# Running the small attention heads of a two-block transformer kernel in pairs on the two halves of the array

## The chip, the cores and the metric

One core of a Trainium2 chip runs the whole program. The metric is device time in microseconds of one execution; the median of three runs of the kernel before is 4096.61 us.

## What is computed

The first block (two mixer layers with attention, gated linear attention and a convolution) stays as it is. The change lies in the second block, in its three kinds of attention heads over 512 positions with heads 64 wide, and in the gates that weigh the three branches afterwards:

```python
def banded_attention(q, k, v, bias_tab, window, sink=None):      # kind B, window 128, with a sink
    s = einsum(q, k) * D ** -0.5 + bias; p = softmax(masked s); return einsum(p, v)

def second_block(...):
    h = rms_norm(x, norm_mix[layer])
    proj = h @ w_in[layer]
    aq, ak, av, bq, bk, bv, cq, ckv, cg, mg = jnp.split(proj, points, axis=-1)
    oa = diff_attention(aq, ak, av, lam, bias_a)      # kind A: 4 heads, p[0] - lam * p[1]
    ob = banded_attention(bq, bk, bv, bias_b, B_WINDOW, sinks[layer])   # kind B: 8 heads, 2 key heads
    oc = nsa_attention(cq, kc, vc, ksel, ckv[:, :, 3], kwin, ckv[:, :, 5], cg, bias_c)
                      # kind C: 8 heads, 2 key heads; g0*o_cmp + g1*o_sel + g2*o_win
    branches = jnp.stack([oa, ob, oc], axis=0)
    y = jnp.einsum('nbsm,nmd->bsnd', branches, w_branch[layer])
    gate = jax.nn.sigmoid(mg.reshape(B, S, N_BRANCH, D_MODEL))
    x = x + jnp.sum(gate * y, axis=2) @ w_out[layer]
```

All is float32. The projections take their operands as two rounded parts each (three products per tile); the scores and the products with the values are plain float32.

## The kernel before

The second block's projections for keys and values come first, then the small compression network, then the stage named "heads", then the branch products (`w_branch_2`), the output projection and the feed-forward part.

**The units of the heads stage.** The stage is a list `heads2` of 160 units, 40 for each of four rounds `i`. A unit is 128 query rows (`qt` 0 to 3) of one head against the keys that these rows may see: 128, 256, 384 or 512 keys for the kinds A (`c0` and `c1`, its two halves), C `sel` and C `win`; 128 or 256 for B; 31 compressed keys for C `cmp`. In a round stand 8 units of A, 8 of B and 24 of C. Before the change the order within B and C is group by group: all four `qt` of key head `g`=0 first, then those of `g`=1. Key head 0 lies on partitions 0 to 63, key head 1 on 64 to 127; likewise the two halves of A.

**What one unit asks of each engine**, all hand-written in order, loop variable `n`:

- TensorE: `scores(n)` multiplies the 64 rows of q and k into one of four PSUM banks (`score_bank`). `turn(n)` transposes the normalised probabilities in 128-column blocks into bank 4 or 5 (line 1540, for `cmp` line 1537). `values(...)` multiplies them by the values and adds up in bank 1; its output takes 64 partitions for B and C.
- VectorE: `maximum(n)` (line 2814) adds the bias and takes the row extreme in one pass over the bank; `normalise(n)` divides (lines 2824 to 2845, line 2235 for a fused form).
- ScalarE: `exp(n)` over the bank, and `copy(n)` of the transposed block to SBUF (both record line 1659).

TensorE runs `scores(n + 3)`, `turn(n)`, any `values`, then the fill of step `n`; VectorE `maximum(n + 2)`, `normalise(n)`; ScalarE `exp(n + 2)`, `copy(n)`.

**The fill.** Between the units TensorE works on 36 projection tiles: 12 query tiles for the following rounds and 24 gate tiles (`mg`). A tile has 8 steps of three 512-column products into bank 2. `planned_fill` spreads the 288 steps at build time over the units, by a cost for each unit (`unit_us`), so that each unit gets an equal share. After a gate tile ScalarE takes its tanh and writes it to DRAM (`gates_kept`); after a query tile it squares and copies, TensorE sums the squares (`mm(bank(2), blk, n2sq, ...)`), and ScalarE takes a logarithm and an exponential. Tanh stands in another function table than the logarithm. Bank 2 is free for the next tile only after that read.

**The weights.** SP loads a tile into one of four ring slots; GpSimd splits it into its two parts (lines 945 and 947) before TensorE may use it.

**After the stage** VectorE computes, for each of 24 branch tiles, `(tanh + 1) * product` and then `0.5 * that` added to the sum (both line 2235, the first branch line 2893).

Of the kernel before, what the change touches and what calls it, by code (L numbers as in the profile page):

```python
# [22 lines left out]
P = 128  # L23
# [203 lines left out]
def two_blocks(nc, a, out, stop=None):  # L227
    ctx = ExitStack()
    with ctx:
# [189 lines left out]
        pT2 = take(3 * LT, LAT, at=KT * ALL)  # L419
# [99 lines left out]
        ms2_read = sem("ms2_read")  # L519
        gate2_tanh, gate2_kept = sem("gate2_tanh"), [sem(f"gate2_kept{j}") for j in range(2)]  # L520
# [9 lines left out]
        for i in range(4):  # L530
            pT_use = 7 * i
            for kind, g, subs in (("A", 0, ("c",)), ("B", 0, ("b",)), ("B", 1, ("b",)),
                                  ("C", 0, ("sel", "win", "cmp")), ("C", 1, ("sel", "win", "cmp"))):
                for sub in subs:
                    for qt in range(LT):
                        lo = max(qt - 1, 0) * P if kind == "B" else 0
                        w = NB2 if sub == "cmp" else (qt + 1) * P - lo
                        for part in ("c0", "c1") if sub == "c" else (sub,):
                            heads2.append(dict(i=i, kind=kind, g=g, qt=qt, sub=part, lo=lo, w=w, turn=turns2,
                                               use=None if sub == "cmp" else pT_use))  # L540
                        turns2 += 1
                    pT_use += sub != "cmp"
# [4 lines left out]
        VALUES_AT = [("A", 0, 8, 2), ("B", 0, 17, 2), ("B", 1, 19, 2), ("C", 0, 28, 3), ("C", 1, 40, 3)]  # L547

        PV_BEFORE = {("A", "c1"): (-1, 4), ("B", 0): (0, 0), ("B", 1): (0, 0), ("sel", 0): (0, 1), ("win", 0): (0, 2),
                     ("sel", 1): (0, 3), ("win", 1): (0, 4), ("cmp", 0): (0, 0), ("cmp", 1): (0, 4)}  # L550

        def values_before(u):

            at, k = PV_BEFORE[("A", "c1") if u["kind"] == "A" else ("B", u["g"]) if u["kind"] == "B" else (u["sub"], u["g"])]
            return max((u["i"] + at) * 5 + k, 0)
# [3 lines left out]
        FILL_TILES, gates_planned = [], 0  # L559
# [8 lines left out]
        def unit_us(n):  # L568

            total = 0.0  # L570
            if n + 3 < 4 * NS2:
                total += 2 * (heads2[n + 3]["w"] / 1200 + 0.1)
            if n < 4 * NS2 and heads2[n]["sub"] != "c0":
                total += 0.1 + 0.11 * -(-heads2[n]["w"] // P)
            for kind, g, first, per in VALUES_AT:
                j, o = divmod(n - first, NS2)
                if 0 <= j < 4 and o < (2 if kind != "C" else 3):
                    total += {"A": 1.1, "B": 0.9, "C": 1.3 if o == 2 else 2.2}[kind]
            return total

        def planned_fill():

            step_us, units = 0.7, 4 * NS2 - 4
            share = (sum(unit_us(n) for n in range(units)) + step_us * KT * len(FILL_TILES)) / units
            plan, ends, at, spent, free = [[] for _ in range(4 * NS2 + 3)], [0] * len(FILL_TILES), 0, 0.0, 0
            for n in range(units):
                spent += unit_us(n)
                while at < KT * len(FILL_TILES) and n >= free and spent + step_us <= share * (n + 1):
                    tile, k = divmod(at, KT)
                    plan[n].append((tile, k))  # L590
                    spent, at = spent + step_us, at + 1
                    if k == KT - 1:
                        ends[tile] = n
                        free = n + (3 if FILL_TILES[tile][0] == "query" else 1)
            assert at == KT * len(FILL_TILES)
            for tile, (kind, q) in enumerate(FILL_TILES):
                if kind == "query":
                    assert ends[tile] + 6 < NS2 * (q // 4 + 1) + (0, 0, 8, 16)[q % 4] - 3
# [4 lines left out]
        def ended(n, kind):  # L603

            return [q for tile, (k, q) in enumerate(FILL_TILES) if k == kind and FILL_END[tile] == n]
# [11 lines left out]
        def pT_slot(use):  # L617

            return use % 3 * LT
# [82 lines left out]
        def _(sp):  # L702
# [279 lines left out]
        def _(pe):  # L982
# [527 lines left out]
            def scores(n):  # L1510
                u = heads2[n]
                b, qs = score_bank(n, u["w"]), qt_[:, u["i"] % 2]
# [12 lines left out]
                mm(b, q, k, True, True).then_inc(scores2, 1)  # L1525
# [17 lines left out]
            def values(i, kind, g, step, per):  # L1543

                mine = [u for u in heads2 if u["i"] == i and u["kind"] == kind and u["g"] == g]
                at = [pT_slot(u["use"]) for u in mine if u["qt"] == 0 and u["use"] is not None]
                rows = slice(g * 64, g * 64 + 64)
                if step == 0:
                    pe.wait_ge(pT2_ready, mine[-1]["turn"] + 1)

                    pe.wait_ge(o2_read, i * 3 + {"A": 0, "B": 1, "C": 2}[kind])
                    if kind == "B":
                        pe.wait_ge(rsA_ready, i + 1)
                steps = []
                if kind == "A":
                    for s in range(LT):
                        steps.append([(bank(1)[:, s * P:], vA[:, s, i * P:(i + 1) * P], pT2[:, at[0] + s, s * P:],
# [12 lines left out]
                if (step + 1) * per >= len(steps):  # L1570
                    last.then_inc(pv2, 1)
# [1387 lines left out]
```

## Time and profile before

| | us |
|---|---|
| median of three runs | 4096.61 (4095.42 to 4098.13) |
| the profiled execution | 4089.71 |
| its span | 4087.9 |
| heads stage, 3093.5 to 3578.4 of the span | 484.9 |
| TensorE busy in the span | 3835.9 (94%) |
| VectorE, ScalarE, GpSimd busy | 1891.2, 1006.2, 1965.8 |
| mean granted TensorE clock | 0.969 |

How to read it: the busy time of TensorE is that of matmul records, which overlap and whose ends are modelled, so the distance from one start to the next tells more than a duration. A plain float32 product is recorded as two matmuls, a transpose or a product of rounded parts as one. The granted clock is 1.00 at 2.4 GHz and 0.50 at 1.2 GHz. A releaser behind an arrow is what the idle time before an instruction ended with.

### The profile page before, as it was taken

The numbers are of one execution on the slowest core, as the hardware profiler recorded it, in microseconds if no ns is written. First come the engines' busy times: TensorE is split into PE (matmuls) and PEld (weight loads), VectorE is DVE, ScalarE is ACT, GpSimd is POOL, SyncE is SP. The second block draws the span as 40 slices with busy tenths as digits, with TensorE's granted clock in tenths as the row PEclk, the third lists the DMA queues.
The fourth block names the chain that finished last, engine by engine and source line by source line (L and its number), as shares of the span: only waits on it lengthen the run. The fifth ranks groups of instructions, "written<-read, shape, count | busy, mean of one in ns | idle before, by whom it ended". The sixth has DMA issues, their size and how long they took to land. (4 is left out here: it accounts for less than half of the span.)

```text
span 4087.9 us, 51442 instructions
## 1 busy us (share of the span) xinstructions
PE 3835.9 (94%) x19551; PEld 3010.5 (74%) x19551; DVE 1891.2 (46%) x2849; ACT 1006.2 (25%) x1824; POOL 1965.8 (48%) x834
## 2 busy tenths in 40 slices
PE   7999999999988998899999999899899999999999
PEld 4777778888877887676678778677585555567877
DVE  3344336556547884244426556456214444463200
ACT  3333112222210001243312222101214444412200
POOL 3333342332335564344454443689443333287886
PEclk9999999999999998999999999999889999999999
DMA  6211221121125553222232222335422222253333
GB/s 207 50 44 48 75 50 42 44 50 42 45 75 118 115 106 108 72 55 56 55 85 55 63 61 51 89 91 140 123 57 69 64 55 68 62 159 78 93 92 92
DMA packets 485314, 317.41 MB, mean 78 GB/s; under 512 B 38185, under 2 KB 456370, under 8 KB 483210
## 3 DMA queue, kind: packets, MB, share of 16 engines
q1 hardware_dynamic: 466080, 288.14, 28.6%
q10 hardware_dynamic: 19050, 26.75, 1.9%
q8 instruction: 124, 2.03, 0.2%
q14 instruction: 60, 0.49, 0.0%
HBM read 282.25 MB, written 32.56 MB: 77 GB/s over the span
## 5 line engine op out<-in xcount | busy, mean ns | idle before, releaser
L945 POOL TENSOR_TENSOR whi<-ring,con 128x1024 fp32r<-128x1024 f32 (+1 forms) x415 | 980.1, 2362 | 2067.1 <-DMA ring<-in_w_in 1596.5
L622 PE MATMUL ps<-xT_parts,whi 128*128 128x512 f32 (+2 forms) x2632 | 1017.2, 386 | 71.7 <-DVE zz L2235 21.1
L622 PE MATMUL ps<-hT_parts,whi 128*128 128x512 f32 (+1 forms) x2864 | 1049.9, 367 | 0.0
L947 POOL TENSOR_TENSOR ring_parts<-ring,whi 128x1024 fp32r<-128x1024 f32 (+1 forms) x415 | 988.9, 2383 | 32.5
L622 PE MATMUL ps<-xT_parts,ring_parts 128*128 128x512 f32 (+2 forms) x2600 | 946.2, 364 | 0.0
L622 PE MATMUL ps<-arena_parts,whi 128*128 128x512 f32 (+1 forms) x2344 | 723.0, 376 | 50.5 <-DVE arena_parts L2267 37.0
L1659 ACT ACTIVATE arena<-ps 128x768 f32<-128x768 f32 (+9 forms) x561 | 298.7, 542 | 1625.9 <-PE ps L622 786.0
L622 PE MATMUL ps<-arena 128*128 128x128 f32 (+9 forms) x3292 | 644.6, 340 | 13.0 <-DVE arena L2235 9.5
L622 PEld LDWEIGHTS ps<-xT_parts,whi 128*128 128x128 f32 (+1 forms) x2632 | 501.2, 190 | 179.0 <-issue 87.9
L622 PEld LDWEIGHTS ps<-hT_parts,whi 128*128 128x128 f32 x2864 | 544.3, 190 | 89.6 <-issue 7.2
L622 PEld LDWEIGHTS ps<-arena 128*128 128x128 f32 (+3 forms) x3292 | 440.4, 194 | 168.3 <-issue 131.4
L622 PEld LDWEIGHTS ps<-xT_parts,ring_parts 128*128 128x128 f32 (+1 forms) x2600 | 492.6, 189 | 85.1 <-issue 0.8
L622 PEld LDWEIGHTS ps<-arena_parts,whi 128*128 128x128 f32 x2344 | 429.5, 192 | 148.1 <-issue 51.9
L622 PE MATMUL ps<-arena_parts,ring_parts 128*128 128x512 f32 (+1 forms) x1312 | 493.1, 376 | 0.0
L622 PEld LDWEIGHTS ps<-arena_parts,ring_parts 128*128 128x128 f32 x1312 | 251.1, 191 | 45.1
L622 PE MATMUL ps<-arena,con 128*128 128x512 f32 (+8 forms) x594 | 214.5, 496 | 41.5 <-ACT arena L1659 40.6
L2235 DVE SCALAR_TENSOR_TENSOR arena<-arena,ps 128x256 f32<-128x256 f32 (+2 forms) x176 | 111.0, 631 | 270.0 <-PE ps L622 228.9
L622 PE MATMUL ps<-whi,xT_parts 128*128 128x256 f32 (+2 forms) x640 | 190.8, 298 | 10.9 <-ACT arena L1659 7.6
L622 PE MATMUL ps<-whi,hT_parts 128*128 128x256 f32 (+2 forms) x640 | 183.8, 287 | 0.0
L622 PE MATMUL ps<-ring_parts,xT_parts 128*128 128x256 f32 (+2 forms) x640 | 183.7, 287 | 0.0
L2235 DVE SCALAR_TENSOR_TENSOR arena<-arena,par 128x512 f32<-128x512 f32 (+2 forms) x83 | 110.9, 1344 | 156.4 <-ACT arena L1659 152.8
L622 PEld LDWEIGHTS ps<-arena,con 128*128 128x128 f32 (+1 forms) x594 | 90.9, 174 | 116.3 <-issue 69.2
(173 smaller groups left out, 3617.7 us busy)
## 6 DMA issues: line engine op xcount, KB each, us to landing
ring<-in_w_in SPq DMA_DIRECT2D x504, 256.0 KB, 4.1
arena<-in_w_ada SPq DMA_DIRECT2D x64, 256.0 KB, 5.8
ring<-in_w_up SPq DMA_DIRECT2D x64, 256.0 KB, 4.0
ring<-in_w_down SPq DMA_DIRECT2D x64, 256.0 KB, 3.9
ring<-in_w_out SPq DMA_DIRECT2D x48, 256.0 KB, 3.9
gates_kept<-stage ACTq DMA_DIRECT2D x24, 384.0 KB, 3.9
arena<-gates_kept SPq DMA_DIRECT2D x24, 384.0 KB, 3.6
arena<-in_w_ada SPq DMA_DIRECT2D x8, 1024.0 KB, 20.0
```

Source lines behind the costliest of these rows:

```text
L622: return nc.tensor.matmul(o, l, r, start=first, stop=last)
L945: v.tensor_tensor(hi, raw, ones[:, 0:m].unsqueeze(1).to_broadcast([P, kt, m]), ALU.mult).then_inc(w_rounded, 1)
L947: v.tensor_tensor(ringR[:, s, 0:kt, 0:m], raw, hi.bitcast(F32), ALU.subtract).then_inc(w_split, 1)
L1659: return nc.scalar.activation(o, i, f, **kw)
L2235: return v.scalar_tensor_tensor(out=o, in0=a0, scalar=s, in1=a1, op0=op0, op1=op1)
```

## The change

The units of a round are put in an order in which neighbours are the two halves of one head (A) or the two key heads of one query tile (B, C `sel`, C `win`); `cmp` keeps its groups apart. All three engines then go through the list two units at a time: TensorE `scores(n + 2)` and `scores(n + 3)` back to back, fill, `turn(n)`, `turn(n + 1)`, values, fill; VectorE both `normalise`, then both `maximum`; ScalarE what is due for a fill tile, then both `exp`, then both `copy`. The products with the values alternate between the two key heads, so that neighbours write the two partition halves of bank 1; there are now six groups of them in a round where there were five. The probabilities lie in a tighter layout (`pT_at`), written block by block. The planner costs a pair as one unit's scores (`pair_us`).

The gate is computed as a sigmoid, exp(-ln(1 + exp(-x))), three ScalarE instructions from the table that the logarithm uses; the branch products use it as it is. The first gate tile is loaded right behind the first four query tiles and multiplied before the first scores.

```diff
-            for kind, g, subs in (("A", 0, ("c",)), ("B", 0, ("b",)), ("B", 1, ("b",)),
-                                  ("C", 0, ("sel", "win", "cmp")), ("C", 1, ("sel", "win", "cmp"))):
-                for sub in subs:
-                    for qt in range(LT):
+            for kind, sub, groups in (("A", "c", (0,)), ("B", "b", (0, 1)), ("C", "sel", (0, 1)), ("C", "win", (0, 1)),
+                                      ("C", "cmp", (0,)), ("C", "cmp", (1,))):
+                for qt in range(LT):
...
+                    for g in groups:
...
-        FILL_TILES, gates_planned = [], 0
+        FILL_TILES, gates_planned = [], 1
...
-                        free = n + (3 if FILL_TILES[tile][0] == "query" else 1)
+                            free = 2 * p + (4 if FILL_TILES[tile][0] == "query" else 2)
...
@@ SP @@
                     for c in range(4):
                         load_query(0, c)
+                    load_gate(0)
...
@@ TensorE @@
+            def scores(n):
+
+                for b, q, k in [operands(n + c) for c in range(2)]:
+                    mm(b, q, k, True, True).then_inc(scores2, 1)
...
-                        steps.append([(bank(1)[rows, s * P:], vS[:, s, rows], pT2[:, at[0] + s, s * P:], s == 0, False)])
-                        steps.append([(bank(1)[rows, s * P:], vW[:, s, rows], pT2[:, at[1] + s, s * P:], False, False)])
+                        for g in range(2):
+                            todo.append((bank(1)[rows[g], s * P:], (vS if kind == "sel" else vW)[:, s, rows[g]],
+                                         pT_keys(use[g], s, s * P, LAT - s * P), kind == "sel" and s == 0, False))
...
+            pe.wait_ge(w_split, splits.number() + 1)
+            for k in range(KT):
+                fill_step(k)
             pe.wait_ge(n2_ready, NORM0 + 4)
-            for n in range(3):
-                scores(n)
-            for n in range(4 * NS2 + 3):
...
+            scores(0)
+            for n in range(0, 4 * NS2 + 2, 2):
+                if n + 2 < 4 * NS2:
+                    scores(n + 2)
                 fill(n)
+                for m in (n, n + 1):
+                    if m < 4 * NS2:
+                        turn(m)
...
+                fill(n + 1)
...
@@ ScalarE @@
+            def gate_value(g):
+
+                product()
+                if g >= 2:
+                    act.wait_ge(gate2_kept[g % 2], 16 * (g // 2))
+                value = gate_out2[g % 2]
+                do(value, bank(2).rearrange("p (a n) -> p a n", a=2), ACT.Exp, scale=-1.0).then_inc(gate2_read, 1)
+                act.wait_ge(gate2_read, g + 1)
+                do(value, value, ACT.Ln, bias=one).then_inc(gate2_ln, 1)
+                act.wait_ge(gate2_ln, g + 1)
+                do(value, value, ACT.Exp, scale=-1.0).then_inc(gate2_ready, 1)
...
@@ VectorE @@
-            for n in range(4 * NS2):
+            for n in range(0, 4 * NS2, 2):
                 i, m = divmod(n, NS2)
+                normalise(n)
+                normalise(n + 1)
                 if n + 2 < 4 * NS2:
                     maximum(n + 2)
-                normalise(n)
+                    maximum(n + 3)
...
-                release(stt(pieces[0], gate_in2[g % 4], 1.0, pieces[1], ALU.add, ALU.mult))
+                release(v.tensor_tensor(pieces[0], gate_in2[g % 4], pieces[1], ALU.mult))
...
-                    v.tensor_scalar(dst, tmp2, 0.5, None, ALU.mult).then_inc(acc_row, 1)
+                    v.tensor_copy(dst, tmp2).then_inc(acc_row, 1)
                 else:
-                    stt(dst, tmp2, 0.5, dst, ALU.mult, ALU.add).then_inc(acc_row, 1)
+                    v.tensor_tensor(dst, dst, tmp2, ALU.add).then_inc(acc_row, 1)
```

How the rows of two engines move. In these rows `ps<-arena 128xN` is a product of scores over N keys (its 64 input rows are not shown), `ps<-con,arena 128x128` a transposed block, `ps<-arena,con 64xN` a product with the values for one key head, and the three names with `_parts` are one fill step.

TensorE, the beginning of the stage, before the change. The first row turns the small gates of kind C.

```order
L622 MATMUL ps<-arena,con 128x96
L622 MATMUL ps<-arena 128x128 x2
L622 MATMUL ps<-arena 128x256 x2
L622 MATMUL ps<-xT_parts,whi 128x512
L622 MATMUL ps<-hT_parts,whi 128x512
L622 MATMUL ps<-xT_parts,ring_parts 128x512
```

And with the change; between the row of the small gates and the first row here stand the 24 products of the first gate tile, of which this shows the last.

```order
L636 MATMUL ps<-xT_parts,ring_parts 128x512
L636 MATMUL ps<-arena 128x128 x2
L636 MATMUL ps<-arena 128x256 x2
L636 MATMUL ps<-xT_parts,whi 128x512
L636 MATMUL ps<-hT_parts,whi 128x512
L636 MATMUL ps<-xT_parts,ring_parts 128x512
```

Eight fill steps moved ahead of the first scores.

TensorE, the first round, kind C, before: one score product at a time, the values of key head 0 alone.

```order
L622 MATMUL ps<-arena 128x512
L1540 MATMUL ps<-con,arena 128x128
L622 MATMUL ps<-arena,con 64x512 x2
L622 MATMUL ps<-arena,con 64x384
L622 MATMUL ps<-arena 128x128
L1540 MATMUL ps<-con,arena 128x128 x2
L622 MATMUL ps<-arena,con 64x384
L622 MATMUL ps<-arena,con 64x256 x2
```

And with the change, at the values of `sel` in the first round.

```order
L636 MATMUL ps<-xT_parts,whi 128x512
L636 MATMUL ps<-hT_parts,whi 128x512
L636 MATMUL ps<-xT_parts,ring_parts 128x512
L1560 MATMUL ps<-con,arena 128x128 x2
L636 MATMUL ps<-arena,con 64x512 x2
L636 MATMUL ps<-arena,con 64x384 x2
L636 MATMUL ps<-arena,con 64x256 x2
L636 MATMUL ps<-arena,con 64x128 x2
```

Each `x2` is now one product for either key head. Counted over the stage, a run of fill steps is followed by scores 117 times before and 56 times with the change; 66 runs then lie between scores and a transpose.

ScalarE, around one gate tile, before, and then with the change.

```order
L1659 ACTIVATE ps,small<-ps,small 128x31 [waits max2]
L1659 ACT_TABLE_LOAD [waits gate2_kept0]
L1659 ACTIVATE hT<-ps 128x2x256 [waits w_used]
L1659 ACTIVATE arena<-ps 31x128 [waits pv2,turned2]
L1659 ACTIVATE ps,small<-ps,small 128x31 [waits max2]
```

```order
L1690 ACTIVATE arena<-ps 128x4x128 [waits pv2,turned2]
L1690 ACTIVATE hT<-ps 128x2x256 [waits w_used]
L1690 ACTIVATE hT<-hT,small 128x2x256 [waits gate2_read]
L1690 ACTIVATE hT<-hT 128x2x256 [waits gate2_ln]
L1690 ACTIVATE small<-small 128x1 [waits max2]
L1690 ACTIVATE ps,small<-ps,small 128x256
```

The table loads of the stage are gone (28 before), and a gate's three instructions stand ahead of the next two exponentials.

## Rows read from the trace of the kernel before

**Rows 1.** Busy time of each engine and granted clock (PEclk) in three stretches.

```profile
core 0: us, PE busy (x) PEld busy (x) DVE busy (x) ACT busy (x) POOL busy (x), PEclk, DMA share, GB/s
3093.50:3101.20 7.70, 4.81 (x16) 3.12 (x16) 4.56 (x15) 3.15 (x10) 5.02 (x2) 0.56 0.00 1
3135.30:3145.60 10.30, 10.11 (x21) 5.45 (x22) 3.74 (x10) 7.40 (x17) 4.69 (x2) 0.50 0.53 159
3093.50:3578.40 484.90, 462.21 (x1794) 274.59 (x1795) 223.44 (x748) 225.54 (x617) 167.55 (x74) 0.96 0.24 61
```

**Rows 2.** Who waited for whom in the heads stage: total us, times, longest.

```profile
DVE ps L2814 <- PE ps L622: 241.3, 141, 8.8
...
ACT ps L1659 <- DVE small L2814: 24.4, 28, 3.3
```

**Rows 3.** TensorE in order of time, kind B: start, duration, tiles, [idle before].

```profile
3152.69 1.12 PE L622 MATMUL ps<-arena 64*128 64x512 f32 x2
3153.75 0.33 PE L1540 MATMUL ps<-con,arena 128*128 128x128 f32 x1
...
3154.85 0.39 PE L622 MATMUL ps<-hT_parts,whi 128*128 128x512 f32 x1
3155.08 0.40 PE L622 MATMUL ps<-xT_parts,ring_parts 128*128 128x512 f32 x1
3155.41 0.48 PE L622 MATMUL ps<-arena 64*128 64x128 f32 x2
3155.83 0.44 PE L1540 MATMUL ps<-con,arena 128*128 128x128 f32 x2
3156.19 0.87 PE L622 MATMUL ps<-arena,con 128*64 128x128 f32 x6
3156.99 0.50 PE L622 MATMUL ps<-xT_parts,whi 128*128 128x512 f32 x1
```

**Rows 4.** TensorE in order of time, kind C: products with the values of one key head.

```profile
3307.73 2.58 PE L622 MATMUL ps<-arena,con 128*64 128x512 f32 x6
3310.23 0.48 PE L622 MATMUL ps<-arena 64*128 64x128 f32 x2
...
3311.02 1.72 PE L622 MATMUL ps<-arena,con 128*64 128x384 f32 x6
3312.67 0.49 PE L622 MATMUL ps<-xT_parts,whi 128*128 128x512 f32 x1
```

**Rows 5.** TensorE in order of time: adjacent products on both halves of the array.

```profile
3038.26 6.08 PE L622 MATMUL ps<-arena,con 128*64 128x512 f32 x16 [0.38 <-DVEq L2229]
...
3096.82 1.72 PE L622 MATMUL ps<-arena 64*128 64x128 f32 x8 [2.75 <-DVE arena L2235]
3098.48 0.79 PE L622 MATMUL ps<-xT_parts,whi 128*128 128x512 f32 x1
```

**Rows 6.** Groups of instructions in the heads stage by form: count, busy us, mean ns.

```profile
L2814 DVE CUSTOM_DVE_ANT_0 ps<-ps,arena 128x512 f32<-128x512 f32 x24 | 16.8, 699 | 30.7 <-PE ps L622 30.5
L2845 DVE TENSOR_SCALAR arena<-ps,small,arena 128x512 f32<-128x512 f32 x16 | 13.0, 810 | 0.7
L1659 ACT ACTIVATE ps<-ps,small 128x512 f32<-128x512 f32 x24 | 15.9, 661 | 8.4 <-DVE small L2814 8.2
L1659 ACT ACT_TABLE_LOAD x16 | 20.5, 1283 | 0.3
L1688 ACT ACT_TABLE_LOAD x12 | 15.4, 1283 | 0.2
```

**Rows 7.** VectorE in order of time: a small operation while GpSimd works (next row).

```profile
3114.01 1.87 DVE L2832 TENSOR_TENSOR small<-small 128x1 f32<-128x1 f32 x1
```

**Rows 8.** GpSimd in order of time: a weight split in the heads stage, two in the branch stage.

```profile
3113.47 2.39 POOL L945 TENSOR_TENSOR whi<-ring,con 128x1024 fp32r<-128x1024 f32 x1 [14.49 <-DMA ring<-in_w_in]
...
3621.18 1.62 POOL L947 TENSOR_TENSOR ring_parts<-ring,whi 128x512 fp32r<-128x512 f32 x1
3622.77 1.29 POOL L945 TENSOR_TENSOR whi<-ring,con 128x512 fp32r<-128x512 f32 x1
```

More of the change, by code:

```diff
@@ L566, in two_blocks, with pair_us @@
                     gates_planned += 1
[L568 to L579, printed above, removed]
+        def pair_us(n):
+            scores = 2 * (heads2[n + 2]["w"] / 1200 + 0.1) if n + 2 < 4 * NS2 else 0.0
+            others = 0.0
+            for m in (n, n + 1):
+                if m < 4 * NS2 and heads2[m]["sub"] != "c0":
+                    others += 0.1 + 0.11 * -(-heads2[m]["w"] // P)
+                for kind, first, steps in VALUES_AT:
+                    j, o = divmod(m - first, NS2)
+                    if 0 <= j < 4 and o < steps:
+                        others += {"A": 1.1, "B": 0.6, "sel": 0.7, "win": 0.7}.get(kind, 0.9)
+            return scores, others
@@ L581, in planned_fill @@
         def planned_fill():
-            step_us, units = 0.7, 4 * NS2 - 4
-            share = (sum(unit_us(n) for n in range(units)) + step_us * KT * len(FILL_TILES)) / units
+            step_us, pairs_ = 0.7, 2 * NS2 - 2
+            steps = KT * len(FILL_TILES)
+            share = (sum(sum(pair_us(2 * p)) for p in range(pairs_)) + step_us * steps) / pairs_
             plan, ends, at, spent, free = [[] for _ in range(4 * NS2 + 3)], [0] * len(FILL_TILES), 0, 0.0, 0
[L586 to L593, printed above, removed]
-                        free = n + (3 if FILL_TILES[tile][0] == "query" else 1)
@@ L595, in planned_fill @@
-            assert at == KT * len(FILL_TILES)
+            for p in range(pairs_):
+                spent += sum(pair_us(2 * p))
+                room = int((share * (p + 1) - spent) / step_us)
+                for slot in range(2):
+                    for _ in range(room - room // 2 if slot == 0 else room):
+                        if at == steps or 2 * p + slot < free:
+                            break
+                        tile, k = divmod(at, KT)
+                        plan[2 * p + slot].append((tile, k))
+                        spent, at, room = spent + step_us, at + 1, room - 1
+                        if k == KT - 1:
+                            ends[tile] = p
+                            free = 2 * p + (4 if FILL_TILES[tile][0] == "query" else 2)
@@ L596, in planned_fill, with ended @@
+            assert at == steps, (at, steps)
             for tile, (kind, q) in enumerate(FILL_TILES):
                 if kind == "query":
-                    assert ends[tile] + 6 < NS2 * (q // 4 + 1) + (0, 0, 8, 16)[q % 4] - 3
+                    assert 2 * (ends[tile] + 4) < NS2 * (q // 4 + 1) + (0, 0, 8, 16)[q % 4] - 2
             return plan, ends
         FILL_PLAN, FILL_END = planned_fill()
-        def ended(n, kind):
-            return [q for tile, (k, q) in enumerate(FILL_TILES) if k == kind and FILL_END[tile] == n]
+        def ended(p, kind):
+            return [q for tile, (k, q) in enumerate(FILL_TILES) if k == kind and FILL_END[tile] == p]
@@ L1541, in turn, with values @@
                 last.then_inc(turned2, 1)
[L1543 to L1547, printed above, removed]
+            def values(i, kind, step, steps):
+                mine = [u for u in heads2 if u["i"] == i and
+                        (u["kind"] == kind or u["sub"] == kind or u["sub"] + str(u["g"]) == kind)]
+                use = {u["g"]: u["use"] for u in mine}
+                rows = [slice(g * 64, g * 64 + 64) for g in range(2)]
@@ L1569, in values @@
+                per = -(-len(todo) // steps)
+                for args in todo[step * per:(step + 1) * per]:
                     last = mm(*args)
-                if (step + 1) * per >= len(steps):
+                if step + 1 == steps:
                     last.then_inc(pv2, 1)
@@ L2119, in _ @@
                 return
+            log_and_exp_table()
             for c in range(4):
```

146 lines of the change are left out of this document (76 added, 70 removed).

## The prediction

> **What bounds the kernel now.** I read the busy table by stretch first, then the waits of the heads stage, then TensorE's instructions in order of time. The change touches one stage of 484.9 us [rows 1]. In it TensorE is recorded busy for 462.2 us, VectorE and ScalarE for some 224 us each, GpSimd for 167.6. VectorE stood idle 241 us for TensorE's scores, 141 times, while ScalarE waited for VectorE only 24 us [rows 2]: the other engines wait for TensorE, so what shortens TensorE's row shortens the stage, until their own chain is as long.
>
> TensorE's row is very regular. A score product runs from its start to the next instruction in 1.06 us at 512 keys and in 0.42 us at 128 [rows 3]; that is 1.67 ns a column and 0.21 us besides, hence 0.63 at 256 and 0.85 at 384. A fill product takes 0.23 us (3154.85 to 3155.08), and the last one before scores 0.33: 0.10 us for the switch. I summed starts to starts over the whole stage in this manner: some 447 us are work and switches, the other 35 us are waits and work at the lower clock.
>
> **The change part by part, against the profiled execution (4089.7 us; the median is 6.9 above it, and the difference is applied to the median).**
>
> *Scores on two row halves.* Do adjacent products on different halves overlap? The chain began with four score products in a row, two of 128 and two of 256 keys, halves alternating: eight records from 3096.82 to 3098.48, 1.66 us [rows 5]. One by one they take 2 x 0.42 + 2 x 0.63 = 2.10 us at the full clock, and that stretch had a granted clock of 0.56 [rows 1], 1.2 GHz at most of it. So each pair cost no more than one product alone. Of the 160 products 128 get such a partner: 16 pairs of 128, 24 of 256, 12 of 384, 12 of 512 keys. Saved: 16 x 0.42 + 24 x 0.63 + 12 x 0.85 + 12 x 1.06 = 44.7 us. The 32 `cmp` products keep their half, but every second one saves the 0.21 us besides the columns: 3.4.
>
> The Trainium skill (TensorE: Matmul & The Clock Gate, Part 3, The mechanism) says that matmuls on different row groups run together, which rows 5 bear out, but also that matmuls start and end in program order without reordering. A float32 product is two records; by that rule the second record of the first product would stand between, a pair would take three steps where one product takes two, and the savings here and in the next paragraph would halve. That is a rival below.
>
> *Values on two column halves.* Sixteen records of 512 columns whose outputs alternate between the partition halves took 6.08 us [rows 5]. In rows 4, on one half, six records of 512, 512 and 384 columns take 2.50 us, which is 0.43 for each of 512, so sixteen would take 6.8 at full clock. Rows 5 lie below that with part of the stretch at half clock, so column halves overlap too. Kind B: six records take 0.80 us (3156.19 to 3156.99 [rows 3]), the 14 of a key head 1.87, eight such 14.9; half is 7.5. Kind C: 2.50 + 1.65 [rows 4] and 0.53 for the last four records of 128, 4.68, eight times 37.4; half is 18.7. Together 26.2 us.
>
> *Fewer switches.* 61 fewer runs of fill go over into scores, at 0.10 us: 6. Products with the values follow a transpose some 20 times less; two blocks go over into them in 0.36 us (3155.83 to 3156.19), 0.14 over their own: 3. With the 3.4 above, 12 us.
>
> *The first gate tile.* Before, TensorE idles 2.75 us ahead of the first scores [rows 5] and then works until 3101.2 at 1.2 GHz. Now 24 fill products (5.5 us) stand there, longer than the gap. The gap goes: 2.75; and the 2.7 us of fill and 1.7 of scores that ran at 0.5 would lose about half: 2. Together 4.7. What it delays: SP now waits at this load for the first query tile's slot before it issues the five bias loads, some 8 us later than now but still over 20 us before the first `maximum`; GpSimd splits the tile (4.8 us) while TensorE has over 15 us of query tiles. ScalarE takes the sigmoid (3 x 0.66) ahead of `exp(0)`; TensorE has the second pair's scores and two fill steps (2.0 us) to cover it, so I cost it at nothing; without that cover it is 2 us, once.
>
> *ScalarE.* 28 table loads of 1.283 us go, 35.9 us [rows 6]. Added are 24 x 2 instructions, at most 0.66 each (the fused exponential of 512 columns [rows 6]), 31.7. So it stays at some 221 us, in a shorter stage 56% busy. Behind the two extra instructions `exp(n + 2)` is queued; its `maximum` is done only some 1.9 us after the pair's scores begin, so little of it shows.
>
> *The shorter look-ahead.* Scores were issued three units ahead and are now one pair ahead; `turn` is where TensorE would wait. For a pair of 512 keys: scores 1.06, then on VectorE 0.70 and 0.14 and the second `maximum`, on ScalarE 0.66 and 0.19 for either, on VectorE reciprocal 0.2 and 0.81 for either [rows 6]: some 5 us from the start of the scores to the second normalised half. TensorE reaches that `turn` after one cycle (397 / 80 = 5.0 us), the next scores and half of a fill, 6 to 7 us. This fits with 1 to 2 us to spare. Against it stand some 15 cycles without fill (behind a query tile the planner leaves a pair free) of 1 to 3 us, and GpSimd: a one-column VectorE operation took 1.87 us until GpSimd's 2.39 us split had ended [rows 7, 8]. I take the waits that remain as large as before (30 us with the low clock): those for bank 2 and for tables get fewer, those at `turn` more. Bounds: 15 less to 45 more.
>
> *The branch stage.* Two VectorE operations per tile change form, none is added. The stage runs at GpSimd's pace, 1.62 + 1.29 us a tile (3621.18 to 3622.77 and on [rows 8]). Zero; if a plain add of two SBUF operands holds GpSimd up more than the fused one, up to 24 x 0.1 = 2.4 us either way.
>
> Sum: 44.7 + 26.2 + 12 + 4.7 = 87.6 us. The stage falls from 484.9 to 397, the profiled execution to 4002, the median to **4009 us**.
>
> **The rivals.** *The chain binds* (11%). Where the cycles without fill expose 2 us of the chain each (30 us) and GpSimd's splits, now in 42% of the stage, hold up every second of the 32 pairs with one-column operations by 1 us (16 us), 46 us come back: 4055. For it: the look-ahead and rows 7. Against it: VectorE's and ScalarE's work is 56% of the new stage.
>
> *Program order inside a pair* (7%): 44.7 + 26.2 come half, 35.4 us less: 4044. Against it: rows 5, where two pairs took less time than four products at full clock; three steps for two would be 1.6 us at the full clock and 2.8 at 0.56, against 1.66 seen. The Trainium skill's sentence on program order (page named above) is what speaks for it.
>
> *No overlap at all behind a fill* (3%): only switches and the start remain: 4080.
>
> *Slower, through the clock* (3%). One mechanism: TensorE waits at `turn` in most pairs, the clock falls to 1.2 GHz in between, and the fill products behind it run at twice their time. It happened in 3135.3 to 3145.6 (granted 0.50 [rows 1]), around the squares of kind A. For a loss over 0.2% it must eat 96 us, so some 190 us of the new stage would have to run at the low level. [...] Against it: the fill now stands on either side of the transposes.
>
> *No difference* (2%): the weights' ring. 36 tiles in 397 us is 11 us for one, while GpSimd needs 4.8 and waited 14.5 us for a landing [rows 8]; it could only be that landing comes late in dense stretches.
>
> **How the numbers follow.** The forecast has 74%; its own range, with waits from 15 less to 28 more, is 3992 to 4037 and holds some 66 of them. Up to 4048 come the rest of its upper side, the second rival and a part of the first: 80 in 100. Below 3992 I leave 5, above 4048 15. Faster by over 0.2% (8 us, about what a measurement of this kernel can tell from no change): 0.74 + 0.11 + 0.07 + 0.03 = 0.95; within: 0.02; slower: 0.03.
>
> **What the profile of the changed kernel would show.** Pairs of score records at the same start within 0.1 us, and a 512-key pair going over into the next instruction in about 1.1 us (1.6 by program order, 2.1 with no overlap). Products with the values of C in 1.3 us where 2.5 stood. No table load in the stage; no idle time of 2.75 us ahead of the first scores and a granted clock of 1.00 there. Waits of TensorE for VectorE's `normalise` lines at about 20 us in all; over 50 would be the first rival. The branch stage as long as before. The prediction is wrong if the stage is longer than 440 us or shorter than 375.

## The result, and the profile of the changed kernel

The changed kernel takes 3996.55 us (median of four runs, 3992.66 to 3999.9), the kernel before, on the same chip, 4096.01. The ratio is 0.9756 (95%: 0.974 to 0.9773): 99.5 us faster, where 87.6 were forecast. The profiled execution of the changed kernel has a span of 3997.1 us.

Busy time by stretch, columns as in [rows 1]: the start of the heads stage with the first gate tile, and the whole stage.

```profile
3098.90:3104.90 6.00, 6.00 (x29) 4.68 (x28) 3.01 (x2) 1.32 (x2) 5.92 (x3) 1.00 0.01 3
...
3098.90:3484.90 386.00, 365.95 (x1796) 239.99 (x1795) 239.55 (x748) 210.65 (x638) 170.71 (x75) 0.99 0.30 76
```

The stage fell from 484.9 us [rows 1] to 386.0, the granted clock in it rose from 0.96 to 0.99. All of the gain lies here. Behind the stage it is 512.2 us now and was 509.5, ahead of it 3098.9 and 3093.5, so the two spans differ by 90.8 us only. Neither is shown to be the change's doing: the profiled run `e1_values_apart`, with the same code behind the stage, takes 509.5 there, and the first score of two profiled executions of the changed kernel starts at 3104.9 and at 3110.8.

TensorE in order of time: a pair of 512 keys, and both heads' products of C `sel`.

```profile
3155.10 1.13 PE L636 MATMUL ps<-arena 64*128 64x512 f32 x4
3156.16 0.50 PE L636 MATMUL ps<-xT_parts,whi 128*128 128x512 f32 x1
...
3165.12 2.38 PE L636 MATMUL ps<-arena,con 128*64 128x512 f32 x16
3167.42 0.50 PE L636 MATMUL ps<-xT_parts,whi 128*128 128x512 f32 x1
```

Two products of 512 keys take 1.06 us from start to next start, what one took in [rows 3]. Sixteen records of C take 2.30 us for both heads; in [rows 4] twelve records of one head took 4.15, and sixteen 4.68 with its last four.

Who waited for whom in the stage (total us, times, longest), to be read beside [rows 2]:

```profile
DVE ps L2860 <- PE ps L636: 84.1, 52, 4.8
...
ACT ps L1690 <- DVE small L2860: 54.7, 26, 5.7
```

VectorE's wait for scores fell from 241.3 to 84.1 us. That is 1.05 us for each of 80 pairs on the mean, but in 52 waits: some pairs have none.

**How the 99 us divide.** I grouped TensorE's records of the stage into runs of one kind and gave each run, at the full clock, the shortest time that the same run took in the traces of these two kernels and of the first eight experiments: that is work with its switches. What lies above it is waiting, or the lower clock. With a smaller set of traces the rows for work and waits shift against each other by up to 3 us. How the rest divides between waiting and the lower clock is less sure: where half of each stretch at the lower clock is counted as its cost, the rows "waits" and "lower clock" read 29 and 15 us before, 26 and 1 in the changed kernel. What the rows leave out, some 19 us in either kernel, is work that stays (kind A's products with the values, sums of squares).

| us, first score to last value | before | changed | gain | forecast |
|---|---|---|---|---|
| scores | 98.7 | 53.5 | 45.2 | 48.1 |
| products with the values | 60.8 | 32.7 | 28.1 | 26.2 |
| fill, with the first gate tile | 220.0 | 214.1 | 5.9 | 6 |
| transposes, kind A's small products | 32.8 | 35.8 | -3.0 | 3 |
| waits | 37.2 | 25.6 | 11.6 | 0 |
| lower clock | 10.0 | 1.0 | 9.0 | 2 |
| gates' product and idle ahead of the first score | 3.2 | 0.2 | 3.0 | 2.7 |

### The profile page after: what moved, and what is told of

It reads as the page before. It is cut to its first block and busy times, and to the rows that moved or that the text cites. A ratio compares the mean times of both kernels' runs of the same rounds, so it can differ in the third digit from the quotient of the medians.

```text
span 3997.1 us, 51466 instructions
## 1 busy us (share of the span) xinstructions
PE 3743.2 (94%) x19551; PEld 2977.4 (74%) x19551; DVE 1908.9 (48%) x2849; ACT 992.3 (25%) x1845; POOL 1966.7 (49%) x834
## 5 line engine op out<-in xcount | busy, mean ns | idle before, releaser
L636 PE MATMUL ps<-arena 128*128 128x128 f32 (+10 forms) x3292 | 590.0, 338 | 10.6 <-DVE arena L2281 6.7
L636 PEld LDWEIGHTS ps<-arena 128*128 128x128 f32 (+3 forms) x3292 | 416.9, 192 | 132.7 <-issue 102.4
L636 PE MATMUL ps<-arena,con 128*128 128x512 f32 (+8 forms) x594 | 184.3, 494 | 36.0 <-ACT arena L1690 35.2
L2592 DVE TENSOR_TENSOR arena<-ps,arena 128x896 f32<-128x896 f32 x160 | 166.2, 1080 | 0.0
```

The source lines that it names most:

```text
L636: return nc.tensor.matmul(o, l, r, start=first, stop=last)
L2592: own(v.tensor_tensor(dst[:, 0:2 * LEVEL_COLS].rearrange("p (l c t) -> p c l t", l=LEVELS, c=2), gE_levels.rearrange("p c (l t) -> p c l t ...
```

## The experiments

Each ratio is to the kernel before, measured beside it; 3996.6 us is the changed kernel. "Stage" is from the first score to the last product with the values: 376.6 us in the changed kernel.

### Do the two row halves run side by side?

```diff
+                both = [operands(n + c) for c in range(2)]
+                for c, (b, q, k) in enumerate(both):
+                    if c == 1 and heads2[n]["sub"] != "cmp":      # the control: c == 0
+                        mm(both[1][0][:, 0:2], ident, ident[:, 0:2], True, True)
                     mm(b, q, k, True, True).then_inc(scores2, 1)
```

The control, with the product ahead of both:

> The changed kernel, plus one product of two columns over the whole array (the identity matrix against two of its columns, overwritten afterwards) ahead of both score products of each of the 64 pairs that are not cmp. It is the control of the run in which the same product stands between the two. Both theories: the halves stay adjacent, so a pair still takes what one product takes (1.06 us at 512 keys). The price is 64 times the small product and a second switch, by the switch of 0.10 us and the fixed 0.1 to 0.2 us of a product some 0.2 to 0.3 us each: 13 to 19 us above the changed kernel's 3996.6, so 4010 to 4016. Less if the waits behind the scores take it up.

The product between the two:

> The same small product over the whole array, now between the two score products of each of the 64 pairs, so that they cannot run side by side on the two row halves. Theory of the prediction (each pair costs one product, overlap worth 44.7 us): 45 us above the control with the product ahead, give or take 6 for switches, so about 4058. Rival, program order inside a pair (overlap worth half of it): 22 us above the control. Rival, no overlap, the gain came from fewer switches and shorter waits: within 5 us of the control. Record starts of a 512-key pair should read 2.1 us or more from the first record to the next instruction, where the changed kernel has 1.06.

Measured: 4006.4 us (ratio 0.9791, 0.9773 to 0.9809) with the product ahead, 9.9 above the changed kernel and a little under what was expected; 4048.1 (0.9897, 0.9864 to 0.9931) with it between: 41.6 us apart, 43.0 in the stage. TensorE, a pair of 512 keys, first with the product ahead, then between:

```profile
3158.01 0.28 PE L636 MATMUL ps<-con 128*128 128x2 f32 x2
3158.22 1.13 PE L636 MATMUL ps<-arena 64*128 64x512 f32 x4
3159.28 0.49 PE L636 MATMUL ps<-xT_parts,whi 128*128 128x512 f32 x1
```

```profile
3163.68 1.12 PE L636 MATMUL ps<-arena 64*128 64x512 f32 x2
3164.73 0.38 PE L636 MATMUL ps<-con 128*128 128x2 f32 x2
3165.04 1.12 PE L636 MATMUL ps<-arena 64*128 64x512 f32 x2
3166.09 0.50 PE L636 MATMUL ps<-xT_parts,whi 128*128 128x512 f32 x1
```

A pair takes 1.06 us from its first start where its records are adjacent, and twice 1.05 where they are not. Work on scores rises from 53.7 to 97.2 us. The full overlap stands; half of it (22 us) and none are out.

### The two column halves, and what passes what

First attempt, apart within a step:

```diff
                 per = -(-len(todo) // steps)
+                for o in range(0, len(todo), per) if kind in ("B", "sel", "win") else ():
+                    todo[o:o + per] = todo[o:o + per:2] + todo[o + 1:o + per:2]
```

> The changed kernel with one edit: within a step, the products with the values of B, C sel and C win are issued for one key head and then for the other, instead of alternating, so that neighbours write the same partition half. Theory of the prediction: the alternation is worth 26.2 us (kinds B 7.5, C 18.7), the part of sel and win of that 7.5 + 16.5 = 24; so 4017 to 4023. Only the one pair at the seam between the heads overlaps. Program order: half, 4008. No overlap on column halves: 3997.

Measured: 4005.7 us (0.9796, 0.9778 to 0.9813), 9 more than the changed kernel by the medians and 3.9 us more in the stage. A miss, and an instructive one. In `sel` and `win` a step now issued, for one head, a product of 512 and one of 384 columns (two records each), and then the same for the other. TensorE's groups by form in the first 0.8 us of such a step:

```profile
L636 PE MATMUL ps<-arena,con 128*64 128x512 f32 x4 | 1.1, 618 | 0.0
```

All four 512-column records begin before any of 384. The second head's first record starts 13 ns after the first head's, past three that were issued ahead of it. So the edit had undone next to nothing in C (2.355 us against 2.304); it bit only in B, where one head has eight records in a step and the other six (28 records in 2.44 us, 1.68 before the edit).

Second attempt, one head whole and then the other, 8 or 14 records each:

```diff
+                if kind in ("B", "sel", "win"):
+                    todo = todo[::2] + todo[1::2]
                 per = -(-len(todo) // steps)
```

> The changed kernel; the products with the values of B, C sel and C win are issued whole for one key head (14 or 8 records) and then whole for the other. In the run before this one, where they were apart only within a step of 8 to 14 records, the trace shows a 512-column product of the second key head start 13 ns after the first head's, although a 384-column product stood between in program order, and C took 2.355 us for 16 records against 2.304. Theory, TensorE lets a product for the other column half pass those before it within a short reach: C's 16 records rise from 2.3 to between 2.8 (reach of about 8 records, as the B steps of the last run point to) and 4.3 (no overlap), B's 28 from 1.68 to 3.0 to 3.6; all in all 11 to 24 us above the changed kernel, 4008 to 4021. Rival, unlimited passing: nothing, 3997 to 4000. The prediction's size for what two column halves are worth in B, sel and win is 24 us: reached only if the overlap is gone.

Measured: 4013.9 us (0.9803, 0.9773 to 0.9832), stage 393.7, 17.1 us more. TensorE in order of time, B and then C `sel`:

```profile
3151.73 2.89 PE L636 MATMUL ps<-arena,con 128*64 128x128 f32 x28
3154.55 0.50 PE L636 MATMUL ps<-xT_parts,whi 128*128 128x512 f32 x1
...
3171.83 3.93 PE L636 MATMUL ps<-arena,con 128*64 128x512 f32 x16
3175.69 0.50 PE L636 MATMUL ps<-xT_parts,whi 128*128 128x512 f32 x1
```

C takes 3.86 us for 16 records and B 2.82 for 28: 8 x 1.55 + 4 x 1.14 = 17.0, the whole difference. Record by record, the second head starts (3173.39) just when three of the first head's eight are left to start, and just three of 14 are left in B as well. What overlap is left can be read off too. The second head alone takes 2.30 us (3173.39 to 3175.69), so two heads one behind the other would take 4.60, 0.74 more than seen; in B it is 3.35, 0.53 more. By this estimate the alternation is worth 17.0 + 8 x 0.74 + 4 x 0.53 = 25 us, where the prediction gave B and C 26.2. (The 24 of the expectations left the last four records of C out.) The run itself shows 17.1 of it.

### The one table

The changed kernel with the gates of before:

```diff
-                do(value, bank(2).rearrange("p (a n) -> p a n", a=2), ACT.Exp, scale=-1.0).then_inc(gate2_read, 1)
-                act.wait_ge(gate2_read, g + 1)
-                do(value, value, ACT.Ln, bias=one).then_inc(gate2_ln, 1)
-                act.wait_ge(gate2_ln, g + 1)
-                do(value, value, ACT.Exp, scale=-1.0).then_inc(gate2_ready, 1)
+                do(value, bank(2).rearrange("p (a n) -> p a n", a=2), ACT.Tanh, scale=0.5).then_inc(gate2_read, 1)
...
                 for q in ended(n // 2 - 2, "query"):
+                    log_and_exp_table()
```

> The changed kernel with the gates as tanh again: one ScalarE instruction for a gate tile, the two function tables with their loads of 1.283 us back, and the branch products' arithmetic of before. Theory of the prediction: 0 us in the stage and in the branch stage (35.9 us of loads against 31.7 us of instructions, off TensorE's path), so 3997 within 4. Theory formed on the trace after: a table load stood between the end of a fill tile and ScalarE's read of bank 2, for which the next tile waits, so the one table is worth 5 to 15 us: 4002 to 4012, with TensorE's waits for ScalarE at hT and n2 groups of fill longer and scores and turn as they are.

The kernel before with the sigmoid of the change, and nothing else of it (the same edit the other way round):

> The kernel before with the gates alone changed: the sigmoid in three instructions of the logarithm's table, no table loads in the stage, the branch products' arithmetic as in the change. The prediction: nothing, 4096 within 3. What undoing it in the changed kernel gave (33 us more, nearly all of it where TensorE waits for bank 2): the loads stood between a tile's end and ScalarE's read of bank 2. With units one by one the trace of before has some 15 us of TensorE's waits at those places; so 10 to 20 us faster, 4076 to 4086.

Measured: 4029.7 us (0.9851, 0.9835 to 0.9868) for the first, 33 more than the changed kernel by the medians and 39 by the ratios, of which 28.7 lie in the stage; 4083.4 us (0.9976, 0.9961 to 0.9991) for the second, 10 less than the kernel before, 13.7 less in the stage. The branch stage moves by less than 2 us in either. Both theories' numbers were too small for the first run. ScalarE and TensorE in order of time at one place of the first round, tanh in the changed kernel:

```profile
3138.41 1.28 ACT L1690 ACT_TABLE_LOAD   x1
...
3139.71 0.69 ACT L1690 ACTIVATE zz<-ps,small 128x512 f32<-128x512 f32 x1
...
3140.41 1.28 ACT L1690 ACT_TABLE_LOAD   x1
...
3142.35 1.28 ACT L1719 ACT_TABLE_LOAD   x1
...
3144.44 0.77 PE L636 MATMUL ps<-xT_parts,whi 128*128 128x512 f32 x1 [5.47 <-POOL ring_parts L962]
```

And the same place in the changed kernel itself:

```profile
3140.21 0.75 ACT L1690 ACTIVATE zz<-ps,small 128x512 f32<-128x512 f32 x1
...
3142.30 0.47 PE L636 MATMUL ps<-xT_parts,whi 128*128 128x512 f32 x1 [1.35 <-issue]
```

The next tile may not begin before ScalarE has read bank 2, and three loads stand ahead of that read: 5.47 us of idle TensorE instead of 1.35. The releaser that the row names, a weight split, is for a later tile: in the changed kernel the same split begins at 3143.21, when this fill already runs. Behind it the clock falls (fill records over 0.4 us apart instead of 0.23). This happens three times, and the other waits behind scores grow likewise: waits in the stage 25.6 to 47.3 us, lower clock 1.0 to 8.3. Two of the three loads are those of kind A's norm, for its logarithm and its exponential. The run has 32 loads in the stage where the kernel before has 28, so it brings back a little more than the change took away.

The Trainium skill (ScalarE: Activation LUTs, What ACT_TABLE_LOAD costs) gives 1283 ns for the load and 1380 ns of drain for each switch. The load agrees with [rows 6]; the drain does not show here: the instruction behind the load starts 1.30 us after the load did (3138.41 to 3139.71).

### How much slack has the chain of VectorE and ScalarE?

Before these runs I had read the slack at the transposes: the time from a pair's first normalised half to its first transpose was 3.3 us at the median, under 0.3 us in 9 of 80 pairs.

```diff
                 if n + 2 < 4 * NS2:
+                    for _ in range(2):                 # range(1) in the other run
+                        own.settle()
+                        own(v.tensor_tensor(*[zz[:, :, LAT:ALL]] * 3, ALU.max))
                     maximum(n + 2)
```

> The changed kernel with two extra VectorE operations of 512 columns (a maximum of an unused tile with itself) in every pair ahead of both maximum operations: the chain from a pair's scores to its second normalised half gets 1.1 to 1.4 us longer in each of the 79 pairs, TensorE gets no work. The prediction gave that chain a slack of 1 to 2 us at the transposes: then some 30 of the pairs would show 0.5 to 1 us of it, 15 to 30 us in all, 4012 to 4027. What the trace of the changed kernel shows, 3.3 us at the median between a first normalised half and its transposes and under 0.3 us in only 9 of 80: 3 to 10 us, 4000 to 4007. The rival, the chain binds already: the whole of it, some 90 us, 4087.

> The changed kernel with one extra VectorE operation of 512 columns in every pair ahead of the two maximum operations, where two of them (1.21 us each, 2.42 a pair) cost 105.5 us in the stage, 1.34 a pair. Theory, VectorE and ScalarE form a loop from pair to pair (maximum, exponential, normalise, next maximum) whose slack is VectorE's wait for scores, 84.1 us in the changed kernel's stage or 1.05 a pair: one operation takes 1.21 of it and exposes 0.16 a pair on the mean, 13 us, and more where pairs are uneven: 15 to 45 us above the changed kernel, 4012 to 4042. Rival, no slack at all and two operations half hidden by chance: half of 105, 4050. Rival, the slack is the 3.3 us at the transposes: 0 to 5.

Measured: two operations 4098.4 us (1.0011, 0.9997 to 1.0024), 102 more than the changed kernel and level with the kernel before; one operation 4036.7 (0.9865, 0.9845 to 0.9885), 38 more than the changed kernel measured beside it (3998.5). The kernel with two, the whole heads stage: who costs VectorE time, who waits, and the stretch.

```profile
L2908 DVE TENSOR_TENSOR zz<-zz 128x512 f32<-128x512 f32 x158 | 191.2, 1210 | 2.7
...
DVE ps L2860 <- PE ps L636: 30.3, 14, 4.3
...
3107.00:3589.20 482.20, 394.56 (x1769) 252.51 (x1768) 398.03 (x901) 206.86 (x632) 172.68 (x73) 0.89 0.24 59
```

The same two rows with one operation:

```profile
L2908 DVE TENSOR_TENSOR zz<-zz 128x512 f32<-128x512 f32 x79 | 81.3, 1029 | 0.0
...
DVE ps L2860 <- PE ps L636: 51.3, 30, 5.8
```

My expectation for the first of them (3 to 10 us) fell flat, and so did the reading behind it. A delay in one pair does not end with its own transposes. VectorE's next `maximum` stands behind its `normalise`, which waits for the exponentials, which wait for the `maximum` before: a loop from pair to pair, and a delay in each round of it adds up until the buffers are used. VectorE's wait for scores is where this loop has room, 84.1 us in the changed kernel, 1.05 a pair on the mean.

The mean does not say what an operation will cost. One operation adds 81.3 us, 1.03 a pair and less than that mean, and yet costs 34.7 us in the stage (0.44 a pair), while 51.3 us of the wait are left. The likely reason is that pairs are uneven: one that had no wait pays in full, and what others have left over does not help it. The second operation adds another 109.9 us and costs 70.8 (0.90 a pair), with 30.3 us of the wait left. Waits and lower clock together are 132 us with two operations where they were 27, about half of it the lower clock. The added operation is not even either: 59 of the 79 took 0.68 to 0.86 us, the other 20 up to 2.7, each of these beside a split of GpSimd. What both steps exclude is 3.3 us of slack, and a chain that binds in every pair, by which one operation would have cost all of its 81 us. That the loop is the reason was read from the order of the instructions; no run takes the loop apart.

### The first gate tile behind the scores

```diff
+            pe.wait_ge(n2_ready, NORM0 + 4)
+            scores(0)
             pe.wait_ge(w_split, splits.number() + 1)
             for k in range(KT):
                 fill_step(k)
-            pe.wait_ge(n2_ready, NORM0 + 4)
-            scores(0)
```

> The changed kernel with the first gate tile's products behind the first pair's scores instead of ahead of them, ScalarE's sigmoid behind the first two exponentials. The prediction: 4.7 us slower (2.75 us idle ahead of the first scores, 2 us of work at the lower clock), 4001. Rival: the first scores wait for the same query tile's norm with or without the tile ahead, but the tile is now a cover behind them, where ScalarE's and VectorE's first units are awaited: 0, 3997. The rows to look at are the idle time ahead of the first score and the granted clock there.

Measured: 4001.8 us (0.9776, 0.9751 to 0.9801), 5.3 above the changed kernel, but the two intervals overlap. TensorE at the first scores of this kernel:

```profile
3112.17 0.80 PE L636 MATMUL ps<-arena 64*128 64x128 f32 x4 [1.40 <-DVE arena L2281]
```

The idle time ahead of them is back, 1.40 us, and the granted clock is 0.5 there, where the changed kernel has no gap and 1.00. From the gates' product on the stage is 2.0 us longer. Gap and clock are as forecast; a difference in time is not shown. Three of its six runs took 3996.8 us, the changed kernel's own time, and the other three 4006.8 to 4012.0.

### Going further

The changed kernel once more, as the measure for these two:

> The changed kernel once more, unchanged, as the measure for the three that share its chip here: every theory gives 3997, give or take the 5 us by which one kernel's times differ.

It took 3998.5 us (0.9771, 0.975 to 0.9792).

```diff
-                                      ("C", "cmp", (0,)), ("C", "cmp", (1,))):
+                                      ("C", "cmp", (0, 1))):
...
-                    todo.append((bank(1)[rows[g], :], vc[0:NB2, g], pTcmp[0:NB2], False, True))
+                    for q0 in (0, 256):
+                        todo.append((bank(1)[rows[g], q0:q0 + 256], vc[0:NB2, g], pTcmp_at(g, q0, 256), False, q0 == 256))
```

> The changed kernel with the units of C cmp paired across the two key heads too (they were paired within one head, on one row half), so their score products lie on two row halves, and both heads' products with the values stand together on two column halves; the second head's transposed probabilities go to a tile of their own. Row halves worth what they were elsewhere: 16 pairs of 31 columns from 0.56 to some 0.3 us, 4; four products of 512 columns behind their neighbour's, 4 x 1.0: 4. Together 8 us below the changed kernel in this call, about 3989. The rival, the loop of VectorE and ScalarE takes it back: within 2 us of it.

Measured: 3995.9 us (0.9764, 0.9745 to 0.9783), 2.6 less, with overlapping intervals. A `cmp` pair's scores now take 0.34 us instead of 0.56 (3.5 in all; behind five of the 16 pairs TensorE waits longer by as much) and the products with the values 4.1 us less, as worked out; but the stage is only 3.7 us shorter. TensorE's wait for the normalised `cmp` probabilities, in the changed kernel and in this one:

```profile
PE ps L1557 <- DVE arena L2281: 1.7, 3, 1.2
```

```profile
PE ps L1559 <- DVE arena L2284: 4.4, 5, 2.4
```

With less work on TensorE at that place the other engines' chain shows: waits took half of it back, as the rival had it.

And on top of that run:

```diff
-                            free = 2 * p + (4 if FILL_TILES[tile][0] == "query" else 2)
+                            free = 2 * p + (4 if FILL_TILES[tile][0] == "query" else 3)
```

> The kernel of the run with cmp paired across the heads, and one number of the planner changed: the fill tile after a gate tile may begin only behind the next pair's transposes, not right behind its scores, where TensorE waits some 14 us in all for ScalarE's read of bank 2. Theory, that wait is covered by the transposes: 5 to 10 us below the run before, about 3982. Rival, the transposes now come before their probabilities are ready, since the fill that covered them is gone: the wait moves to the transposes, no gain or up to 10 us of loss.

Measured: 3992.5 us (0.9748, 0.973 to 0.9767), 6.0 below the changed kernel measured beside it. TensorE's idle time between scores and fill falls from 14.6 to 10.3 us, but 3.2 come up ahead of transposes, and the stage is only 1.3 us shorter than in the run before. The fastest kernel of this study, though its interval and the changed kernel's overlap: a lead of some 6 us that these runs do not prove.

## Why the prediction was right, and where it was off

- **Scores on two row halves, 44.7 us.** Right: 41.6 us between the two runs with the small product, 45.2 in the sum above. The view that carried it was [rows 5], two pairs in less time than four products one by one. The 3.4 us for `cmp` were half that: a pair on one half takes 0.56 us where two single ones took 0.67.
- **Values on two column halves, 26.2.** Right: 28.1 in the sum above, some 25 for B and C by the run with whole heads. It went by [rows 3] and [rows 4] halved, and both heads of B take 1.68 where half of two heads gives 1.87.
- **Fewer switches.** 6 us for fill right (5.9). The 3 us for transposes did not come: the row with A's small products rose by 3.0, which is also what the method can shift. No run tried the switches alone.
- **The first gate tile, 4.7.** The gap went, and the start has the full clock (1.00). With the tile behind the first scores the stretch from the gates' product on is 2.0 us longer; a difference in the kernel's time is not shown.
- **ScalarE at nothing.** This is the step that failed. I set 35.9 us of loads against 31.7 us of instructions on an engine that is half idle, and took the difference for the price. What the price hangs on is where they stand: 24 of the 28 loads stood right ahead of ScalarE's reads of bank 2, on TensorE's path. On the kernel before one table is worth 10 us (13.7 in the stage), in the changed kernel 33 or more. Why it is three times as much was not tried: the pairs put these reads ahead of both exponentials, TensorE has less work to cover a wait, and that run has four loads more. Without the one table the change would have gained some 61 to 66 us, not 99.
- **Look-ahead and waits, unchanged at 30 (15 less to 45 more).** The base was too low: the table has 47.2 us of waits and lower clock in the stage before where the prediction counted 35. Measured 20.6 less for the two together, 18.6 of it beyond the 2 us forecast for the start: just outside the lower bound, by no more than the method's 3 us. It is the same step: 13.5 us of it is what one table alone took off waits and low clock in the kernel before.
- **The slack, 1 to 2 us a pair.** The size was right by luck. The prediction looked at the transposes, and there it is 3.3 us; VectorE's wait for scores is 1.05 a pair on the mean. But one operation of 1.03 us a pair already costs 35 us in the stage, so the rival *the chain binds* was closer than "1 to 2 us to spare" says. TensorE's waits for `normalise` lines, promised at about 20 us, are 4.5 on the rows of its products and 20.8 on those of its weight loads.
- **Program order inside a pair** fell: 41.6 us between the two runs where it gave 22. The Trainium skill's sentence that spoke for it (TensorE: Matmul & The Clock Gate, Part 3, The mechanism: "strict FIFO, no reordering") does not hold in these traces for products on different halves: records of the second product of a pair start beside the first's, and in the values a record passed three that were issued earlier.
- **Slower through the clock** was not near in the changed kernel (0.99), but its mechanism exists: with two more operations in the loop the clock in the stage was 0.89 and the kernel level with the one before.
- **The branch stage** as forecast, no change (its first 600 records take 167.6 us in both kernels).

The total came out well since the misses partly met: 7 us less work saved than forecast, 19 us more of waits and low clock gone.

## What to carry to other kernels

Let neighbouring products use different halves of the array: here a float32 pair on two row or two column halves cost one product, and on column halves an order that was off by three records still overlapped. Before costing an engine's instruction at nothing because the engine is half idle, ask whose buffer it reads or frees: a table load ahead of such a read is on the bound engine's path. Look for the slack of a software pipeline where the other engines wait for the bound one, and pair by pair, not at the place where a result is used: here 3.3 us at the use said nothing, and even the mean of 1.05 us at the wait was too kind, since 1.03 us more in each pair already cost 35 us.

## What the runs showed of the hardware

- In these traces TensorE lets a product for the other column half start ahead of three earlier records, and no more: starts 13 ns apart with three records between, and a start exactly when three were left where there were eight (C) or 14 (B).
- A full-array product of two columns between two half-array ones takes 0.31 us, start to start; ahead of a pair, behind fill, 0.21.
- A one-column VectorE addition in B's chain took 790 ns on the mean of 32, where it takes 150 to 160 undisturbed: 15 of them took over 500. VectorE in the changed kernel's stage, by form:

```profile
L2870 DVE TENSOR_TENSOR small<-small 128x1 f32<-128x1 f32 x32 | 25.3, 790 | 6.9 <-ACT ps L1690 6.9
```

With GpSimd's splits now in 171 of 386 us, these are what [rows 7] showed once. All 15 overlap a split and end within 0.15 us of its end; of the other 17 only one lies beside a split for over 0.1 us. A run without the splits was not made.
